# A mixture-of-experts stage in blocks of 32 tokens instead of 64, one weight load per expert

## The reference, cut to what matters

```python
h = rmsnorm(x, norm_ffn_g)
logits = h @ w_router + b_router                  # 288 x 32
top_vals, top_idx = lax.top_k(logits, 4); gates = softmax(top_vals)
for each expert e, for its tokens xb:             # w_up[e] 1024 x 2048, w_down[e] 1024 x 1024
    gate, up = split(xb @ w_up[e] + b_up[e])      # 1024 and 1024 columns
    gate = minimum(gate, 7); up = clip(up, -7, 7)
    act = (up + 1) * gate * sigmoid(1.702 * gate)
    y[token] += gates[token, e] * (act @ w_down[e] + b_down[e])
out = rmsnorm(x + y, norm_final_g)
```

## Time and profile before

| what | value |
|---|---|
| median of 3 runs | 1427.42 us (1427.17 to 1430.05) |
| span of the profiled execution | 1428.9 us |
| mean granted clock of TensorE | 0.973 of full speed |
| busy PE / PEld / DVE / ACT | 1376.0 / 755.0 / 526.6 / 229.9 us |
| read from HBM | 459.32 MB |
| first matmul of the expert stage | 406.3 us |

### The profile page before, as it was taken

The page is one execution under the profiler, slowest core; times in us unless marked ns, Lnnn a source line. Parts: engine busy times, 40 slices in busy tenths (PEclk is TensorE's granted clock), DMA queues, the critical chain, the costliest instruction groups (busy, mean ns, idle before and its releaser), DMA issues.

```text
span 1428.9 us, 19236 instructions
## 1 busy us (share of the span) xinstructions
PE 1376.0 (96%) x7048; PEld 755.0 (53%) x7048; DVE 526.6 (37%) x1195; ACT 229.9 (16%) x346; POOL 54.5 (4%) x70
## 2 busy tenths in 40 slices
PE   5899989998799999999999999999999999999996
PEld 4777767776554444454444454444554444544443
DVE  1698861221414332234232234222243322343324
ACT  3012122102111111111111111111111111111112
POOL 0253200000000000000000000000000000000000
PEclk9899999999579999999999999999999999999999
DMA  8943423343049999999999999999999999999990
GB/s 257 340 151 121 134 78 121 119 142 130 12 186 378 406 411 412 416 414 414 405 415 414 416 410 416 405 414 417 413 409 416 408 415 412 417 410 414 409 399 33
DMA packets 115584, 461.19 MB, mean 323 GB/s; under 512 B 8494, under 2 KB 46446, under 8 KB 81723
## 3 DMA queue, kind: packets, MB, share of 16 engines
q1 hardware_dynamic: 115166, 459.02, 81.4%
q10 hardware_dynamic: 349, 1.04, 0.2%
q0 software_dynamic: 48, 0.85, 0.2%
HBM read 459.32 MB, written 2.42 MB: 323 GB/s over the span
## 4 chain that ended last, share of the span: by engine, by line
PE 88%; DVE 8%; POOL 2%; ACT 1%; DMA 0%; issue 0%; SPq 0%; DVEq 0%; ACTq 0%
PE bank L1096 32%; PE bank L1127 16%; PE bank L915 13%; PE bank L932 13%; PE bank L922 6%; DVE R L665 5%; PE bank L897 5%; POOL prod L451 1%; POOL big L434 1%; PE bank L1081 1%; DVE R L674 1%; PE bank L1054 1%; DMA vecrows<-in_norm_ffn_g 0%; PE bank L991 0%; PE bank L1013 0%
## 5 line engine op out<-in xcount | busy, mean ns | idle before, releaser
L1096 PE MATMUL bank<-ring,big 128*64 128x512 f32 x2112 | 463.3, 597 | 0.0
L1096 PEld LDWEIGHTS bank<-ring,big 128*64 128x64 f32 x2112 | 149.3, 137 | 292.0 <-issue 292.0
L1127 PE MATMUL bank<-ring,R 128*64 128x512 f32 x1056 | 233.9, 595 | 0.0
L915 PEld LDWEIGHTS bank<-R,stage 128*128 128x128 f32 x1632 | 192.2, 196 | 28.3 <-issue 28.3
L915 PE MATMUL bank<-R,stage 128*128 128x64 f32 x1632 | 198.0, 279 | 0.0
L932 PE MATMUL bank<-hT,ring 128*128 128x288 f32 x768 | 192.9, 413 | 2.8 <-DVE WT L630 1.4
L848 DVE COPY big<-bank 128x512 f32<-128x512 f32 x33 | 22.8, 692 | 405.3 <-PE bank L1096 405.3
L932 PEld LDWEIGHTS bank<-hT,ring 128*128 128x128 f32 x768 | 147.6, 194 | 44.4 <-DVE WT L630 1.8
L1127 PEld LDWEIGHTS bank<-ring,R 128*64 128x64 f32 x1056 | 72.9, 137 | 156.9 <-issue 156.9
L305 DVE TENSOR_TENSOR xt<-xt,bank 128x512 f32<-128x512 f32 (+1 forms) x204 | 124.3, 676 | 7.1 <-PE bank L922 7.1
L665 DVE SCALAR_TENSOR_TENSOR R<-big,convw,R 128x256 f32<-128x256 f32 x240 | 99.8, 494 | 0.0
(11 more groups left out here) (178 smaller groups left out, 584.2 us busy)
## 6 DMA issues: line engine op xcount, KB each, us to landing
ring<-in_w_up SPq DMA_DIRECT2D x264, 1024.0 KB, 11.5
ring<-in_w_down SPq DMA_DIRECT2D x132, 1024.0 KB, 7.6
ring<-in_w_in SPq DMA_DIRECT2D x24, 1024.0 KB, 10.5
ring<-in_w_branch_b SPq DMA_DIRECT2D x4, 1024.0 KB, 4.9
ring<-in_w_branch_a SPq DMA_DIRECT2D x4, 1024.0 KB, 5.0
ring<-in_w_out SPq DMA_DIRECT2D x4, 1024.0 KB, 5.0
xt<-in_x_prompt SPq DMA_DIRECT2D x2, 512.0 KB, 3.8
out_y_prompt<-xt SPq DMA_DIRECT2D x2, 512.0 KB, 2.7
```

The lines of the kernel that those rows point to most:

```text
L915: ins = mm(XB[:, k * BLK:(k + 1) * BLK], stage[:, tt, k * P:(k + 1) * P], sel[:, tt, :], start=tt == 0, stop=tt == NT - 1)
L1096: ins = mm(dst[q * BLK:(q + 1) * BLK, :], xT[:, k, :], ring[:, k, lo:lo + 512], start=k == 0, stop=k == UP_SLOTS - 1)
L1127: ins = mm(DN[q * BLK:(q + 1) * BLK, :], lhsT, ring[:, k, lo:lo + 512], start=f == 0, stop=f == KC - 1)
```

## The change

Blocks have 32 tokens. The items are sorted by expert, so the blocks of an expert follow each other, and SP loads an expert once: it waits until the *last* block of the expert before has used a slot (`items_before` gives the number of blocks before it). `up_used` and `down_used` count the slots used.

A block's hidden rows are now 32 wide, and four matmuls lie side by side in the array, each on 32 of its columns: `up` puts the four groups of 512 `w_up` columns into four quarters of bank UP, `down` puts two halves of the contraction and two halves of the output columns into the four quarters of DN. Gathering turns round: `sel` (32 columns) is the stationary operand and `stage` moves, 256 columns a matmul; the gathered rows are copied by ScalarE (`take_rows`) and turned by two transposes (`turn_rows`). The raw up result is one bank: one copy, four transposes, one bias add. `combine` contracts 64 rows, in which the two halves of the down contraction are summed; rows that hold nothing are zeroed once by GpSimd.

The loop body of TensorE starts after a block's up projection. It gathers the next block, turns the raw result, combines row tiles 1 and 2 of the block before, turns rows and weights, does this block's down projection whole, and then the next block's up projection, with row tile 0's combine behind its fourth slot.

The bias `b_down` comes in as an item of its own: it is loaded into `out_sb` and combined with the gates of all tokens. The tables of ranks and gates go; `select` and `select_weighted` compare with an offset into `slot_ids` instead (the round's first rank, from the item's column). At the end, norm and store go row tile by row tile.

The core of the diff; of the pieces marked with only + signs the old lines stand in the functions above:

```diff
 TOPK = 4
-BLK = 64
+BLK = NE
+QN = P // BLK
 MAX_ROUNDS = -(-T // BLK)
-TBL = MAX_ROUNDS * NE
 MAX_ITEMS = NE + (T * TOPK) // BLK
+COLUMN_MAX = MAX_ROUNDS * NE - 1
+ROUND_BITS = 15 * NE
 SLOTS = 12
 SLOT = 2048
 UP_SLOTS = 8
+DOWN_SLOTS = SLOTS - UP_SLOTS
...
         bank = [ctx.enter_context(nc.psum_tensor(f"bank{i}", [P, 512], F32)) for i in range(8)]
-        U0, U1, T0, T1, XB, DN, Y0, Y1 = bank
+        UP, TB, Y2, Y3, XB, DN, Y0, Y1 = bank
+        row_banks = ((Y0, Y1), (Y2, Y3), (Y0, Y1))
+        tail_banks = ((Y0, Y1), (Y2, Y3), (UP, XB))
...
+            def load_slot(e, k):
+
+                if k < UP_SLOTS:
+                    src = a["w_up"][0, bass.ds(e, 1), k * P:(k + 1) * P, :].rearrange("e p n -> (e p) n")
+                    dst = ring[:, k, :]
+                else:
+                    j = k - UP_SLOTS
+                    src = a["w_down"][0, bass.ds(e, 1), j * 256:(j + 1) * 256, :].rearrange(
+                        "e (h p) n -> p (e h) n", p=P)
+                    dst = ring[:, k, :].rearrange("p (h n) -> p h n", h=2)
+                sp.dma_start(dst, src).then_inc(slot_full[k], 16)
+
+            for k in range(SLOTS):
+                sp.wait_ge(*mix_block_used(MIX_BLOCKS - SLOTS + k))
+                load_slot(0, k)
             sp.wait_ge(items_known, 1)
-            count = sp.value_load(n_items[0:1, 0:1], min_val=NE, max_val=MAX_ITEMS)
-            expert_reg = sp.alloc_register("expert")
-            with sp.Fori(2, count) as i:
-                column = sp.value_load(items[0:1, bass.ds(i, 1)], min_val=0, max_val=TBL - 1)
-                sp.reg_alu(expert_reg, column, NE - 1, ALU.bitwise_and)
-                load_expert(sp.snap(expert_reg, min_val=0, max_val=NE - 1), i * SLOTS - (SLOTS - 1))
+            with sp.Fori(1, NE) as e:
+                before = sp.value_load(items_before[0:1, bass.ds(e - 1, 1)], min_val=0, max_val=MAX_ITEMS)
+                for k in range(UP_SLOTS):
+                    sp.wait_ge(up_used, before * UP_SLOTS + (k + 1))
+                    load_slot(e, k)
+                for j in range(DOWN_SLOTS):
+                    sp.wait_ge(down_used, before * DOWN_SLOTS + (j + 1))
+                    load_slot(e, UP_SLOTS + j)
...
+            def take_rows(i):
+
+                act.wait_ge(gathered, i + 1)
+                nc.scalar.copy(xg, XB[:, 0:256]).then_inc(rows_ready, 1)
+
+            def take_raw(i):
+
+                act.wait_ge(up_used, i * UP_SLOTS + UP_SLOTS)
+                nc.scalar.copy(raw, UP[:, :]).then_inc(raw_ready, 1)
+
+            def finish(i):
+
                 act.wait_ge(g1_ready, i + 1)
+                nc.scalar.activation(sg.rearrange("p (c t) -> p c t", c=4), lin.rearrange("p (c t) -> p c t", c=4)[:, :, 0:64],
+                                     ACT.Sigmoid, scale=ALPHA).then_inc(sig_ready, 1)
+                act.wait_ge(combT_turned, i + 1)
+                nc.scalar.copy(combT, TB[:, 0:NT * P]).then_inc(combT_ready, 1)
+                act.wait_ge(down_used, i * DOWN_SLOTS + DOWN_SLOTS)
                 act.wait_ge(combined, i * NT + NT)
                 nc.scalar.copy(out_sb, DN[:, :]).then_inc(out_ready, 1)
+
+            take_rows(0)
+            act.wait_ge(items_known, 1)
+            bodies = act.value_load(n_bodies[0:1, 0:1], min_val=NE - 1, max_val=MAX_ITEMS - 1)
+            with act.Fori(0, bodies) as i:
+                nc.scalar.activation(ss[:, 15:16], eps_col[:], ACT.Sigmoid)
+                take_raw(i)
+                take_rows(i + 1)
+                finish(i)
...
                 for tt in range(NT):
+                    ins = V.tensor_scalar(comb[:, tt], slot_ids[:, bass.ds(rank0, BLK)].unsqueeze(1).to_broadcast([P, QN, BLK]),
+                                          rankm[:, tt, bass.ds(expert, 1)], gates[:, tt, bass.ds(expert, 1)],
+                                          ALU.is_equal, ALU.mult)
                 ins.then_inc(comb_ready, 1)
 
+            def take_x(i):
+
+                dve.wait_ge(rows_turned, i + 1)
+                V.tensor_tensor(xT, XB[:, 256:512].rearrange("p (k t) -> p k t", k=KC),
                                 cols[:, NORM_FFN, :].unsqueeze(2).to_broadcast([P, KC, BLK]), ALU.mult
                                 ).then_inc(xT_ready, 1)
...
+            def activate(i, column):
+
+                dve.wait_ge(raw_turned, i + 1)
+                bias = bupT[:, bass.ds(column & (NE - 1), 1), :].rearrange("p e f -> p (e f)")
+                V.tensor_tensor(lin.rearrange("p (f t) -> p f t", f=16), TB[:, :].rearrange("p (f t) -> p f t", f=16),
+                                bias.unsqueeze(2).to_broadcast([P, 16, BLK]), ALU.add).then_inc(biased, 1)
+                dve.wait_ge(biased, i + 1)
+                V.tensor_scalar(lin3[:, :, 0:64], lin3[:, :, 0:64], LIMIT, None, ALU.min).then_inc(g1_ready, 1)
+                V.tensor_scalar(lin3[:, :, 64:P], lin3[:, :, 64:P], LIMIT, -LIMIT, ALU.min, ALU.max).then_inc(u1_ready, 1)
...
+            def swish(i):
+
+                dve.wait_ge(g1_ready, i + 1)
                 dve.wait_ge(sig_ready, i + 1)
+                V.tensor_tensor(gs3, lin3[:, :, 0:64], sg3, ALU.mult).then_inc(gs_ready, 1)
+                dve.wait_ge(u1_ready, i + 1)
+                dve.wait_ge(gs_ready, i + 1)
+                V.scalar_tensor_tensor(actT.rearrange("p c q t -> p c (q t)"), lin3[:, :, 64:P], 1.0, gs3, ALU.add, ALU.mult
+                                       ).then_inc(act_ready, 1)
...
+            def add_before(i):
+
+                for tt in (1, 2):
+                    dve.wait_ge(combined, i * NT + (tt + 1))
+                    add_output(dve, row_banks[tt], tt)
+
+            with dve.Fori(0, bodies) as i:
+                column, column1, column2 = (
+                    dve.value_load(items[0:1, bass.ds(i + n, 1)], min_val=0, max_val=COLUMN_MAX) for n in range(3))
+                activate(i, column)
+                take_x(i + 1)
+                swish(i)
+                dve.wait_ge(combT_turned, i + 1)
+                select_weighted(column1)
                 dve.wait_ge(gathered, i + 2)
+                select(column2)
+                add_before(i)
+                dve.wait_ge(combined, i * NT + (NT + 1))
+                add_output(dve, row_banks[0], 0)
+            activate(bodies, dve.value_load(items[0:1, bass.ds(bodies, 1)], min_val=0, max_val=COLUMN_MAX))
+            swish(bodies)
+            add_before(bodies)
...
+            def scale_rows(tt):
+
+                dve.wait_ge(rooted, 6 + tt)
+                V.reciprocal(ss[:, 4 + tt:5 + tt], ss[:, 4 + tt:5 + tt]).then_inc(sums_added, 1)
+                dve.wait_ge(sums_added, 2 + tt)
+                V.scalar_tensor_tensor(xt[:, tt, :], xt[:, tt, :], ss[:, 4 + tt:5 + tt], fing, ALU.mult, ALU.mult
+                                       ).then_inc(y_ready, 1)
...
+            for tt in range(NT):
+                dve.wait_ge(combined, bodies * NT + (NT + tt + 1))
+                add_output(dve, tail_banks[tt], tt)
+                if tt >= 1:
+                    scale_rows(tt - 1)
+            scale_rows(NT - 1)
...
-            def gather(tiles):
-
-                for k in tiles:
-                    for tt in range(NT):
-                        ins = mm(XB[:, k * BLK:(k + 1) * BLK], stage[:, tt, k * P:(k + 1) * P], sel[:, tt, :],
+            def gather():
+
+                for tt in range(NT):
+                    for q in range(QN):
+                        ins = mm(XB[q * BLK:(q + 1) * BLK, 0:256], sel[:, tt, :], stage[:, tt, q * 256:(q + 1) * 256],
                                  start=tt == 0, stop=tt == NT - 1)
-                return ins
-
-            def combine(tt):
-
-                for q in range(2):
-                    ins = mm(row_banks[tt][q][:, :], combT[q * BLK:(q + 1) * BLK, tt * P:(tt + 1) * P],
-                             out_sb[q * BLK:(q + 1) * BLK, :], start=True, stop=True)
+                ins.then_inc(gathered, 1)
+
+            def turn_rows(i):
+
+                pe.wait_ge(rows_ready, i + 1)
+                turned = XB[:, 256:512].rearrange("p (q h t) -> p h q t", q=QN, h=2)
+                for h in range(2):
+                    ins = tr(turned[:, h], xg[:, h * P:(h + 1) * P])
+                ins.then_inc(rows_turned, 1)
+
+            def combine(tt, banks):
+
+                for h in range(2):
+                    ins = mm(banks[h][:, :], combT[64 * h:64 * h + 64, tt * P:(tt + 1) * P],
+                             out_sb[64 * h:64 * h + 64, :], start=True, stop=True)
                 ins.then_inc(combined, 1)
...
+            pe.wait_ge(sel_ready, 1)
+            gather()
+            turn_rows(0)
+
+            pe.wait_ge(bdown_in, 32)
+            pe.wait_ge(combT_ready, 1)
+            combine(0, row_banks[0])
+            pe.wait_ge(listed, 1)
+            tr(Y3[0:1, 0:P], item_column).then_inc(list_turned, 1)
+
+            def up(k, fills):
+
+                pe.wait_ge(slot_full[k], fills)
```

(130 more changed lines are left out.)

271 lines of the change are left out of this document (72 added, 199 removed).

## The result

The changed kernel takes 1474.01 us (median of 4 runs, 1473.09 to 1477.50) against 1428.74 (4 runs, 1427.17 to 1430.37) of the kernel before, measured beside it: ratio 1.0322, 95% interval 1.0310 to 1.0335. It is slower by 3.2%; forecast were 1464.5 us and 2.6%.

What follows compares the result with a forecast made beforehand. Weight transfers bound the kernel, their queues running empty once per multi-block expert: start to 426.3, cycles 1009, last block's work and tail 17.5 + 13.5 gave 1466 us of span, 1464.5 in the runs; range 1440 to 1532.

Steps and rivals of the forecast that it cites:

- rival 1: TensorE's narrow matmuls: only two tiles run at a time, group 1.72 us, 1926 us in all; chance 0.06.
- rival 3: TensorE's groups of four overlap imperfectly, three at a time: group 1.15 us, 1558 us in all; chance 0.10.
- rival 4: A 32-column matmul is cheaper than its moving columns; at half the time 1431 us, no change; chance 0.04.
- estimate of 1.08: Us per group of four tiles at the Trainium skill page's efficiency of 0.79, instead of the 0.86 taken.
- resident block: TensorE's work on one block with all weights present in the ring: 17.6 us, 35.2 for two.
- middle: From the end of a block's up to its down's start: 6.0 us, bounds 5.0 to 7.0.
- One-block cycles: Last-slot landing of a one-block expert to that of the next: queue never empties, 30.1 us, 12 times.
- pairs behind multi-block experts: Landing-to-landing times of two-block experts that follow a multi-block one: TensorE ends them at 35.2 us, 8 times.
- hand-over: DMA queues empty from a multi-block expert's last byte until its last block's first up slot: 4.4 us, bounds 3.4 to 5.0.
- pairs behind a one-block expert: Landing-to-landing times of two-block experts that follow a one-block one: bound by transfers at 34.6 us, 8 times.
- the transfer loop: One expert's transfers of 30.1 us plus 4.4 of idle queues and 0.1 of issue steps: 34.6 us.
- rival 2: The clock falls in streamed phases, where a slot brings 0.86 us of work each 2.5: adds 66 us, 1532; chance 0.10.

Runs made afterwards that it cites:

- experiment 4: Changed kernel with TensorE turning the gathered rows before combine 1 and 2 instead of behind them: 1461.90 us, ratio 1.0234 to the kernel before.
- experiment 1: Changed kernel leaving out every block after an expert's first, so 32 blocks and 32 loads: 1347.75 us.
- 3: Changed kernel with each expert slot's transfer after expert 0 cut to its first 32 partitions, a quarter of the bytes: 1313.14 us.
- 5: Changed kernel with the next block's up slots 0 to 3 before this block's down projection, 4 to 7 behind: 1426.98 us, ratio 0.9991 to the kernel before.
- 6: Changed kernel with four up slots before the down projection and rows turned before combine 1 and 2: 1421.08 us, ratio 0.9953 to the kernel before.
- the versions of 7 to 10: Changed kernel with rows turned first and two, six, one or three up slots before the down projection: 1413.72, 1443.96, 1426.46 and 1411.63 us.
- experiment 11: Changed kernel with one block per expert and each group of four up and down matmuls issued twice: 1346.03 us.
- experiment 2: Changed kernel with the weights loaded again for every block, 51 loads after the first: 1946.14 us.

## Why the prediction was right, and what was off

**Right.** The mechanism, the sign and the time of a group. A group of four tiles takes 0.858 us (predicted 0.86; rivals 1, 3 and 4 are out, and so is the prediction's estimate of 1.08). A resident block takes 17.54 us (17.6), its middle 5.83 (6.0), set by `take_x`: VectorE waits 0.88 us for L913 at 735.60 with the sigmoid done, and experiment 4 moves the middle to 4.97 by turning the rows first. One-block cycles were 30.1, all 12. The eight pairs behind multi-block experts summed to 280.9 (8 x 35.2 = 281.6), expert 2 took 52.5 (52.7), and expert 1 took 35.1 (36.5). That the cause is the hand-over and not the bytes or TensorE's amount of work is shown from three sides: no multi-block experts (experiment 1), no transfers to wait for (3), the same loads and the same matmuls with most of the hand-over gone (5, 6 and the versions of 7 to 10). The split also shortens a block, from 17.54 us to 16.85; but experiments 4 and 6, whose resident blocks take 16.68 and 16.58 us, still lie 41 us apart, and that is the hand-over.

**Mis-sized: the pairs behind a one-block expert**, 8 x 34.6 = 276.8, "the transfer loop". They took 285.0, 8.2 more, and TensorE ended them. The step that failed is the middle, which I took as one number for all blocks. Behind a streamed up it is 7.0, so the down projection ends later than the landing of the last slot would have it: 35.1 a pair (experts 5, 7, 10, 27) instead of the 34.6 that experiment 4 shows where that middle is 6.1. This is half of the 8.2 us. The other half is rival 2 in small: four of the eight (experts 14, 18, 20, 23) met the lower clock in the last up slot or the gather of their first block and took 35.8, 36.6, 35.7 and 36.5. I had put rival 2 at 66 us, as if the clock stayed low through whole middles; it cost about 4 (in experiment 4 it cost the same pairs 2). The clock did fall, for 6.8 to 13.7 us during the load of every expert behind a one-block one (expert 1 excepted), but mostly where the wait for transfers hid it. By the Trainium skill ("TensorE: Matmul & The Clock Gate", Part 1) the lower level is the default and activity lifts it; experiments 1 and 11 agree (0.86 and 1.00 in the same stretch).

**Start and end.** First up came at 389.80 (391.8), but expert 1 landed at 425.8 (426.3): most of its bytes were in by 423.8, and one of the 16 DMA engines went on to 425.3. From there to expert 31's landing at 1440.7 it took 1014.9 us (1009), and from that to the end 30.8 (31.0). Sum: -0.5 at the start, +6 in the cycles, -0.2 at the end: a span of 1471.5 for 1466. The +6 is the 8.2 above, less 1.4 at expert 1 and 0.7 at the pairs behind multi-block experts, so errors of my sum cancel in a small part.

**Span and time.** I took 1.5 us off the span, as the profiled execution of before lay above the median. After, the profiled run lay under it: 1473.25 us for a span of 1471.5, median 1474.01. That is 4 of the 9.5 us by which the forecast missed. A time here is its span and 1.7 to 1.9 us; the rest was the chance of which run was profiled.

## What to carry to other kernels

When a buffer ring holds exactly one set of weights and a set is used more than once, look at which use frees the first slot: the queues are idle from the last landing until then, once per set. Moving three of eight slots of that use ahead of the work that waits for the last landing bought 3.4% here; moving six gave most of it back. Work out the cost of the same piece of code twice, resident and streamed: behind a wait, register loads that otherwise run ahead lie open (7.0 for 5.83 us here), and the clock may be lower.

## Of the hardware

- Four float32 tiles of 32 columns, started together, take 0.858 us for 512 moving columns. That is 2 records at 0.84 ns per column, the time per column of the full-width matmuls and of two tiles of 64 in the earlier trace rows.
- From 430 to 1320 experiment 1, with 0.86 us of up matmuls in each 2.5 us of a streamed up, had a mean granted clock of 0.86; experiment 11, with 1.72 us, had 1.00. Both moved 418 GB/s.
- The register loads on line 1152 leave TensorE idle for 0.95 to 0.98 us behind an up that waited for its last slot, and for nothing in a resident block; without them (experiment 2) the gather follows at once.
- A transfer into idle queues had its first packet 1.0 us after its issue (741.93 to 742.91, and 391.97 to 392.97) and landed 4.8 us after it. In the second place only a quarter of the DMA engines were busy at first; the full flow began at 393.65.
